# Choice of keys and levels of linear attention beside the projections' tiles, and attention's scores three heads ahead

## The reference, cut to what matters

```python
h = rms_norm(x, norm1_g)
(qa, ka, va, qi, ki, wi, qb, kb, vb, rb, gl, uc) = split_cols(h @ w_in)
# qa, ka, qi, ki are rotated by position (partial_rope)
# a) attention, 8 heads, over chosen keys: per block of 128 queries
score = sum_h wi * relu(qi @ ki.T) * IDX_SCALE          # 4 index heads
_, idx = lax.top_k(where(causal, score, -inf), 128)     # n_keep = min(256, 512 // 4)
o_a = softmax(where(valid, q @ k[idx].T * ATTN_SCALE, -inf)) @ v[idx]
# b) gated linear attention, 4 heads: S_t = diag(a_t) S_{t-1} + k_t^T v_t, o_t = q_t S_t,
#    log a = log_sigmoid(gl @ w_gate_up + b_gate) / 16; then rms norm, times silu(rb)
# c) multiscale_pool(uc)
x = x + concat([o_a, o_b, o_c]) @ w_out
x = x + conv_glu_ffn(rms_norm(x, norm2_g))
```

## Time and profile before

| what | us |
| --- | --- |
| median of three runs (5285.48 to 5310.4) | 5291.39 |
| the profiled execution, its own time | 5324.58 |
| its span, first to last instruction | 5322.7 |
| first layer: projections | 18.07 to 209.22 |
| first layer: mixers | 209.22 to 428.40 |
| second layer: projections | 963.78 to 1154.82 |
| second layer: mixers | 1154.82 to 1379.63 |

### The profile page before, as it was taken

One profiled execution on the slowest core, in us unless ns is written; L12 is line 12 of the kernel. 1 busy time (PEld: TensorE's weight loads), 2 busy tenths in 40 slices (PEclk: granted clock), 3 DMA queues, 4 the chain that ended last, 5 costly groups with the idle time before them and its releaser, 6 DMA issues.

```text
span 5322.7 us, 63196 instructions
## 1 busy us (share of the span) xinstructions
PE 4985.8 (94%) x27502; PEld 2773.6 (52%) x27502; DVE 1481.4 (28%) x2779; ACT 1077.8 (20%) x2068; POOL 324.2 (6%) x302
## 2 busy tenths in 40 slices
PE   9879999987899999999998988888999999989999
PEld 4444444444444444665554567777544555544444
DVE  2362210227211010000224346664310334410100
ACT  1121000012100012110214133333211333311210
POOL 1110000101000000000004100000000001000000
PEclk9879999987899999999999999998999999989999
DMA  3222222223122111111134322210311000101211
GB/s 130 87 111 79 72 71 77 75 79 121 70 79 74 67 57 63 48 48 48 60 127 133 130 66 72 69 54 26 125 52 54 18 26 26 41 31 65 87 71 56
DMA packets 91842, 378.39 MB, mean 71 GB/s; under 512 B 7984, under 2 KB 33712, under 8 KB 62128
## 3 DMA queue, kind: packets, MB, share of 16 engines
q1 hardware_dynamic: 80608, 332.92, 17.6%
q0 software_dynamic: 9808, 37.75, 2.1%
q10 hardware_dynamic: 1152, 3.67, 0.2%
HBM read 334.46 MB, written 39.85 MB: 70 GB/s over the span
## 4 chain that ended last, share of the span: by engine, by line
PE 70%; DVE 4%; ACT 2%; issue 2%; DMA 0%; POOL 0%; POOLq 0%; DVEq 0%; ACTq 0%
PE ps L521 29%; PE ps L333 21%; PE ps L542 5%; PE ps L3335 2%; PE ps L1748 2%; PE ps L3262 1%; PE ps L339 1%; PE ps L3346 1%; PE ps L2445 1%; PE ps L3265 1%; PE ps L3261 1%; PE ps L2395 1%; PE ps L948 1%; PE ps L3263 1%; PE ps L1779 0%
## 5 line engine op out<-in xcount | busy, mean ns | idle before, releaser
L521 PE MATMUL ps<-A,W 128*128 128x512 f32 (+1 forms) x5408 | 2178.4, 563 | 23.4 <-DVE A L1670 6.2
L521 PEld LDWEIGHTS ps<-A,W 128*128 128x128 f32 x5408 | 1032.6, 192 | 1126.4 <-issue 1084.3
L333 PE MATMUL ps<-A,W 64*64 64x64 f32 (+3 forms) x3264 | 710.3, 386 | 44.5 <-DVE R L2886 13.8
L333 PE MATMUL ps<-A 64*64 64x64 f32 (+3 forms) x8416 | 510.5, 246 | 73.2 <-ACT A L3488 23.2
L333 PEld LDWEIGHTS ps<-A,W 128*128 128x128 f32 (+2 forms) x3264 | 397.3, 168 | 337.9 <-issue 308.7
L333 PEld LDWEIGHTS ps<-A 64*64 64x64 f32 (+2 forms) x8416 | 467.8, 155 | 182.3 <-issue 103.7
L542 PE MATMUL ps<-W,A 128*128 128x512 f32 (+1 forms) x896 | 366.7, 572 | 2.2 <-ACT A L1534 2.2
L542 PEld LDWEIGHTS ps<-W,A 128*128 128x128 f32 x896 | 173.5, 194 | 193.6 <-issue 187.8
L435 ACT ACTIVATE A<-R 128x512 f32<-128x512 f32 (+1 forms) x96 | 52.6, 574 | 790.3 <-DVE R L1544 356.0
L1664 DVE SCALAR_TENSOR_TENSOR A<-ps,V,A 128x512 f32<-128x512 f32 (+1 forms) x48 | 31.0, 660 | 486.9 <-PE ps L333 486.3
L1544 DVE SCALAR_TENSOR_TENSOR R<-ps,MOD,R 128x512 f32<-128x512 f32 (+1 forms) x48 | 31.7, 662 | 440.8 <-PE ps L521 439.5
(11 more groups left out here) (356 smaller groups left out, 4253.9 us busy)
## 6 DMA issues: line engine op xcount, KB each, us to landing
W<-in_ada SPq DMA_DIRECT2D x48, 1024.0 KB, 5.4
W<-in_w_up SPq DMA_DIRECT2D x44, 1024.0 KB, 4.8
W<-in_w_down SPq DMA_DIRECT2D x32, 704.0 KB, 4.0
W<-in_w_in SPq DMA_DIRECT2D x18, 1024.0 KB, 4.8
W<-in_sgu_v SPq DMA_DIRECT2D x16, 1024.0 KB, 4.8
W<-in_sgu_u SPq DMA_DIRECT2D x16, 1024.0 KB, 4.8
W<-in_sgu_z SPq DMA_DIRECT2D x16, 1024.0 KB, 4.8
W<-in_sgu_o SPq DMA_DIRECT2D x16, 1024.0 KB, 4.8
```

What stands on the lines that cost most here:

```text
L333: r = e.matmul(out, a, b, start=start and i == 0, stop=stop and i == len(pairs) - 1, skip_group_check=loose)
L521: t = e.matmul(ps, w[:, k, c:c + mc], x(k, seg), start=k == 0, stop=k == kt - 1)
```

## The change

The diff does these things, in both layers of the first block.

* The tiles of the projections get the order qi (2), ki, gl and wi, qb, kb, qa (4), ka (4), uc (2), rb (2); then vb (4 tiles), then va (4). So w_vb is loaded ahead of w_va. They use banks 0 to 3 alone.
* From tile 5 (kb) on, each of the 21 tiles has a place `beside` it: for block j = 1 to 3, seven tiles, of which the first holds the four index heads and the next six the rounds of the choice (3, 3, 3, 3, 2, 2), and each of the 21 one step of linear attention. These use banks 4 to 7. The barrier between projections and mixers is gone, and buffers are laid so that these parts may overlap: `b.h` lies on `b.mix`, `b.tmp` on `b.pr`, the gate's scratch on `b.pt`, and each query block has its own mask.
* The mixers' turns run from -3 to 31. PE makes the transposes of t first and then the scores of t + 3; ACT and DVE are two ahead. `index` and `chosen` are gone from the turns, and linear attention starts there at its step 22, the chunk 2 of 4.
* POOL's two window averages (`pool_mix`) come after all its products for linear attention.

```diff
+QI, KI, GL, GQ, GK, QA, KA, UC, RB, VB, VA, TILES = 0, 2, 3, 4, 5, 6, 10, 14, 16, 18, 22, 26
+ROPED = (0, 1, 2, 6, 7, 8, 9, 10, 11, 12, 13)
+FIRST = 5
+ROUNDS = (3, 3, 3, 3, 2, 2)
+def beside_tile(m):
+    return ((m - FIRST) // 7 + 1, (m - FIRST) % 7) if m >= FIRST else (0, 0)
 def block1_sp(pl, e, l):
...
+    slab_load(pl, e, ("w_vb", l), ins["w_vb"][l])
     for i in range(2):
         slab_load(pl, e, ("w_va", l, i), ins["w_va"][l, i])
-    slab_load(pl, e, ("w_vb", l), ins["w_vb"][l])
...
+    def beside(m, seg=None):
+        r = m - 1
+        if r in ROPED:
+            ps = take(pl, ("rot", l, r), ring)
+            e.wait_ge(*S_.act_projected.at(l, r))
+            e.wait_ge(*free(pl, ("rot", l, r)))
+            e.matmul(ps[:, :], table(pl, "rot"), b.dest[r], start=True, stop=True).then_inc(
+                *S_.rotated.next((l, r)))
+        j, part = beside_tile(m)
+        if j:
+            for hh in range(4 if part == 0 else 0):
+                index(j, hh)
+            next(strand)
...
-    end(pl, ("proj", l), "pe")
-    mixers_pe(pl, e, l)
+    mixers_pe(pl, e, l, strand)
...
+    for m in range(TILES):
+        if m < VB and m not in (GL, GQ):
...
+        j, part = beside_tile(m)
+        if j:
+            for hh in range(4 if part == 0 else 0):
+                index(j, hh)
+            next(strand)
+    mixers_act(pl, e, l, strand)
...
-    end(pl, ("proj", l), "dve")
-    for event in ends(pl, ("proj", l)):
-        e.wait_ge(*event)
-    mixers_dve(pl, e, l)
+        j, part = beside_tile(m)
+        if j:
+            for hh in range(0 if part else 4):
+                index_dve(pl, e, l, j, hh)
+            next(strand)
+            if part:
+                select_dve(pl, e, l, j, part - 1)
+    mixers_dve(pl, e, l, strand)
...
-TURNS = range(-2, 33)
-ROUNDS = (3, 3, 2, 2, 2, 2, 2)
+TURNS = range(-3, 32)
...
-            if x == "s" and 0 <= t + 1 < 32:
-                scores(t + 1)
+            if x == "s" and 0 <= t + ahead < 32:
+                scores(t + ahead)
...
-            elif x == "i":
-                for hh in heads:
-                    index(j, hh)
-            elif x == "r" and 0 <= t < 24 and t % 8 < 7:
-                chosen(t // 8 + 1, t % 8)
...
-    mixers(pl, e, l, scores, turned_, index, nothing_of, gla_pe, ada, pooled, nothing_of, weighed, "stiagow")
+    mixers(strand, scores, 3, turned_, ada, pooled, nothing_of, weighed, "tsagow")
...
-    mixers(pl, e, l, scores, turned_, index, nothing_of, gla_act, ada, pooled, nothing_of, weighed, "stigaow")
+    mixers(strand, scores, 2, turned_, ada, pooled, nothing_of, weighed, "stgaow")
...
-    mixers(pl, e, l, scores, nothing_of, index, chosen, gla_dve, ada, nothing_of, probs, nothing_of, "sriagp")
+    mixers(strand, scores, 2, nothing_of, ada, nothing_of, probs, nothing_of, "sagp")
...
-def mixers_pool(pl, e, l):
+def gla_pool(pl, e, l):
...
-        if lev == 1:
-            pool_mix(pl, e, l, 0)
+        yield
+        yield
...
-    pool_mix(pl, e, l, 1)
+    yield
```

More of the change, by code:

```diff
@@ L548, in tokens_pe @@
                 pl.slab_freed[key] = S.projected.last()
+        if beside is not None:
+            beside(i)
 def merged(work):
@@ L654, in block1_pe, with index @@
         inputs_in(pl, e)
[L656 to L663, removed]
+    strand = gla_pe(pl, e, l)
+    ring = "0123"
+    def index(j, hh):
+        L, o, at = P * (j + 1), 64 * (hh % 2), ("index", l, j, hh)
+        ps = take(pl, at, "4567")[:, 0:L]
+        if (j, hh) == (1, 0):
+            e.wait_ge(*S_.roped.at(l, KI))
+        e.wait_ge(*free(pl, at))
+        e.matmul(ps, b.qi[o:o + 64, hh // 2, P * j:P * j + P], b.ki[o:o + 64, 0:L], start=True, stop=True).then_inc(
+            *S_.index_scores.next((l, j, hh)))
+    def beside(m, seg=None):
[11 more added lines that the diff above has]
+            next(strand)
     h = lambda k, s: b.h[:, k, :]
[L666 removed]
+    features_pe(pl, e, ("w_in", l), [("w_in", l, 0)], 8, 256, h, [(0, S)], beside=beside, ring=ring,
                 ready=lambda k, s: S_.normed.at(("n1", l), k, SC))
[L668 to L670 removed]
+    features_pe(pl, e, ("w_in", l), [("w_in", l, 1)], 8, 256, h, [(0, S)], begun=KI, keep=True, beside=beside, ring=ring)
+    wv = slab(pl, ("w_in", l, 1), 2048, 8)
+    ps = take(pl, ("wi", l), "4567")
     e.wait_ge(*free(pl, ("wi", l)))
@@ L789, in block1_pool @@
     e.memset(b.uc[:, :, 0:16], 0.0).then_inc(*S_.pool_zeroed.next(("uc", l)))
+    strand = gla_pool(pl, e, l)
     e.wait_ge(*S_.rope_ready.at(l, "c"))
[L791 to L795, removed]
-        e.wait_ge(*event)
-    mixers_pool(pl, e, l)
+    for x in b.uy:
+        e.memset(x[:, 0:16], 0.0).then_inc(*S_.pool_gla.next())
+    for m in range(TILES):
+        r = m - 1
+        if r in ROPED:
+            e.wait_ge(*S_.rotated.at(l, r))
+            e.tensor_tensor(b.dest[r], b.dest[r], b.CT, ALU.mult).then_inc(*S_.pool_roped.next((l, r)))
+        if beside_tile(m)[0]:
+            next(strand, None)
+    pool_mix(pl, e, l, 0)
+    pool_mix(pl, e, l, 1)
     end(pl, ("mixers", l), "pool")
@@ new lines, in select_dve @@
+def select_dve(pl, e, l, j, part):
+    S_, b, L, wrote = pl.S, pl.b1[l], P * (j + 1), pl.S.dve_wrote
+    sc, wk = b.sc[:, 0:L], b.wk[:, 0:L]
+    if part == 0:
+        e.wait_ge(*S_.index_summed.last())
+        e.tensor_tensor(sc[:, L - P:L], sc[:, L - P:L], table(pl, "causal"), ALU.add).then_inc(*wrote.next())
+    for rnd in range(ROUNDS[part]):
+        src = sc if part == 0 and rnd == 0 else wk
+        e.wait_ge(*wrote.last())
+        e.max(b.m8, src).then_inc(*wrote.next())
+        e.wait_ge(*wrote.last())
+        e.match_replace(wk, b.m8, src, USED).then_inc(*wrote.next())
+    if part == len(ROUNDS) - 1:
+        e.wait_ge(*wrote.last())
+        e.tensor_scalar(b.bias[j], wk, USED, NEG, ALU.not_equal, ALU.mult).then_inc(*S_.selected.next((l, j)))
```

207 lines of the change are left out of this document (91 added, 116 removed).

## The result

| what | us |
| --- | --- |
| median before (5285.48 to 5310.4), the runs beside those of after included | 5300.65 |
| median after (5159.72 to 5183.07) | 5172.74 |
| the profiled execution of after, its own time and its span | 5159.72, 5157.9 |

The ratio is 0.976, with a 95% interval of 0.9723 to 0.9797: 128 us less. The forecast was 5190 us, 101 less, with a range of 5135 to 5255.

The account below looks back on a forecast made before the run. PE was taken to bound the projections, each turn's chain and a low clock the mixers. Projections 218.6 plus mixers 141 gave 359.6 us per layer against 410.3, 101 less for two layers: 5190 us, range 5135 to 5255.

Parts of the forecast that it names:

- Projections: Projections stage, per layer: 191.15 us plus 18 of moved PE work, 6.5 of waits and 3 for the clock, 218.6.
- the part that was put at 3.6 us: PE work moved beside the tiles: linear attention's gate, one transposition and the first of four chunks, estimated at 3.6 us.
- The waits: PE's waits in projections: second index group 1.5 us, last level 2, keys' transposition 1, second chunk 2; 6.5 in all.
- DVE's load: DVE in the projections: busy time up to some 120 us, the moved work fitting beside the tiles at some 80% load.
- the rival: Beside the tiles DVE becomes late, partly through POOL contention: two us at 21 places, 5255 us, or 5290; chance 0.12.
- Mixers, work that stays: Mixers: of PE's 117 us at full clock 18 move beside the tiles and 99 stay.
- Mixers, waits: Mixers: PE waits about 8 us at the start, 3 at the norm, 3 in the last three turns; 14 together.
- The doubt about a drain: Start of the mixers: by the skill page table switches drain 1.38 us each, making the forecast 5.6 us later.
- Mixers, the clock: Mixers: PE's granted clock rises from 0.73 to 0.78, so 99 us of work take 127.
- The rival of the full clock: Mixers: denser PE work keeps 2.4 GHz, 75 us less per layer, 5140 us; chance 0.18.
- The chain not shortened: Mixers' turns: PE still late by one engine each turn, mixers 165 us, 5238 us in all; chance 0.18.
- half clock throughout: Mixers: PE stays at 1.2 GHz, mixers 208 us, 5324 us in all, slower by 0.6%; chance 0.07.

Follow-up runs that it names:

- Experiment 5: The changed kernel with each max of the choice made twice on DVE, beside the tiles; 5177.76 us, ratio 0.9757 to the kernel before.
- experiment 6: The changed kernel with DVE's division ahead of its step of linear attention in each turn; 5166.23 us, ratio 0.9748 to the kernel before.
- experiment 7: The changed kernel with the spread rows of the norm before the projections in banks 4 to 7; 5164.99 us, ratio 0.9743 to the kernel before.
- 1: The changed kernel with scores one head ahead again on all engines, the moved work still beside the tiles; 5218.71 us, ratio 0.9848 to the kernel before.
- 3: The changed kernel with linear attention back in the turns, only the choice beside the tiles; 5243.92 us, ratio 0.9895 to the kernel before.
- 4: The changed kernel with index scores and choice back in the turns, only linear attention beside the tiles; 5229.49 us, ratio 0.9863 to the kernel before.
- experiment 9: The changed kernel with six idle DVE max instructions before the divisions of pairs 13, 20 and 26; 5189.57 us, ratio 0.9793 to the kernel before.

## Why the prediction was right, and where its sizes were off

**Projections, forecast 218.6, measured 217.59 and 217.46: right in the sum, and partly by luck.** PE's busy time was to be 191.15 + 18 + 3 for the clock, 212.2; it is 211.93. The two terms behind it were both off. The granted clock did not fall against before: it is 0.97 against 0.96, and in the second layer 0.96 against 0.95. Busy time times clock, added up over windows of 1 us, gives 184.3 us of work at full clock before and 205.1 after, 20.8 more (181.4, 202.4 and 21.0 in the second layer). So the moved work took some 21 us and not 18, and the 3 us for the clock did not come; the two errors cancel. Most of the first is the part that was put at 3.6 us: gate, transposition and chunks take 6.0 (1.09 at 81.26, 0.60 at 212.41, twice 0.59 for L1054, and 1.54 and 1.62 for the products at 227.01 and 237.35), since not one but two chunks have their products there. The mixers lost only some 16 us of work by the same reckoning; why it is 5 us less than what came in here isn't shown.

The waits were to be 6.5; the windows leave 217.59 - 211.93 = 5.7. Three of the four places were right in kind: 2.5 us at a level's product behind ACT's relu of the second index group (forecast 1.5), 1.8 at the last level (2), 1.3 at the second chunk (2), and none at the transposition of the keys (1). The clock behind such a wait is seen in the next group:

```profile
199.20 1.17 PE L1032 MATMUL ps<-A 32*128 32x128 f32 x32 [1.78 <-POOL A L1388]
200.30 12.27 PE L542 MATMUL ps<-W,A 128*128 128x256 f32 x32
200.00:202.00 2.00, 2.00 (x21) 1.59 (x14) 1.61 (x3) 0.00 (x0) 0.00 (x0) 0.69 0.00 0
202.00:204.00 2.00, 2.00 (x6) 1.55 (x6) 1.93 (x6) 0.00 (x0) 0.00 (x0) 0.50 0.00 0
```

The second line joins the last sixteen products of vb, of 256 columns, with the first sixteen of va, of 512. Such groups take 3.72 us (at 193.69) and 7.13 (at 228.49) at full clock, 10.85 together, so the low clock cost some 1.4 us. Most of what the clock takes from the stage stands behind no wait at all: during and behind 64 products of only four columns (10.64 us from 54.09 on, PE busy throughout) the clock is 0.80 and 0.68 in the two windows of 10 us from 51.31 on, and the kernel before has the same at its own 64, which start at 154.08: 0.50 from 158 to 168.

**DVE's load, forecast up to 120 us in the stage: right.** It is 117.52 and 121.89. Where the tiles carry moved work, from 80 to 238.9, DVE is busy 106.4 of 158.9 us, 67% and not the 80% of the forecast. The index sums with 512 keys took 752 ns on average, as against 1.33 us for the two of the earlier trace rows; but POOL was idle while they ran (194.16 to 196.62), so they are no test of the contention that spoke for the rival. A large DVE operation with two inputs that did meet a POOL product, L1325 at 207.62, took 0.92 us, where the eleven operations of the same size in L821 took 0.69. Experiment 5 settles the rival: DVE has room for 25 us more.

**Mixers, work that stays, forecast 99 us: right.** 115.22 x 0.88 is 101.4.

**Mixers, waits, forecast 14 us, measured 12.7: right in the sum.** The start has 6.9 us of idle PE up to 267.5 with the norm within it (forecast 8 and 3, so 4 too many): 1.6 at the chunk that opens the stage, 0.6 at a division, 1.8 at the norm's roots and 2.9 at the division behind the norm's end, which experiment 6 could only push on to ACT's copy. The last three turns wait 1.18, 0.78 and 0.69 us for the copy and w_out 0.52, 3.2 in all (forecast 3). The other 2.6 us are short waits inside the turns, for which nothing was forecast. Only one of the two tables was loaded there, for 1.28 us at 239.31, with ACT idle for another 1.08 us behind it; the silu table had been loaded at 228.90, beside the tiles. The doubt about a drain (the Trainium skill, ScalarE: Activation LUTs, "What ACT_TABLE_LOAD costs") doesn't come into the result, since ACT waits for DVE at that place in any case; the load starts 0.02 us after the ACTIVATE ahead of it, and the 1.08 us behind it are less than the 1.38 that the prediction took from the page, so this load shows no such drain either.

**Mixers, the clock, forecast 0.78, measured 0.88: this is the term that was mis-sized.** 99 / 0.78 was 127 us, measured are 115.2: 12 of the 13 us by which the mixers came out shorter, in each layer. The 0.88 lies above the 0.75 to 0.85 that the prediction named as what the profile would show (and the bare turn of 3.02 us just above its 2.6 to 3). In the other kernels whose mixers are those of after the clock was 0.85 and 0.84 (experiment 5), and 0.81 and 0.89 (7): never as low as 0.78. The stage cut at its joints:

```profile
238.90:249.40 10.50, 8.94 (x37) 5.33 (x35) 4.78 (x18) 4.35 (x14) 0.00 (x0) 0.63 0.32 136
249.40:267.50 18.10, 12.80 (x115) 7.23 (x114) 6.76 (x20) 7.74 (x17) 0.00 (x0) 0.88 0.61 233
267.50:296.00 28.50, 27.67 (x114) 11.53 (x114) 6.30 (x34) 9.19 (x31) 1.33 (x2) 0.67 0.49 181
296.00:366.80 70.80, 65.81 (x409) 36.38 (x409) 22.88 (x86) 28.95 (x75) 7.80 (x8) 1.00 0.59 225
```

I took a mixture of the two levels from the earlier trace rows for the whole stage. What came is both in a row: up to 296, with the short turns of 128 and 256 keys and with waits of 1.6 to 2.9 us, something between 0.63 and 0.88; from there to the end the full level, 2.4 GHz, even over the last turns with their idle gaps up to 1.18 us. The stretch at 359 of before, on which I leaned against the full clock, was no sample of these turns. The rival of the full clock, 5140, was right for the last 71 of 128 us and wrong for the rest.

**The sum.** Forecast were 101 us less in four stages, measured are 135: 26 of the 34 are the mixers' clock and waits in two layers, 2 the projections, and 5.5 the second layer's worse start (415.9 against 410.3), which I had not counted. By medians 128 us are gained and not 135; 3.2 of the difference are the first tile's wait, the rest is no more than what medians of a few runs leave open. That the time itself was met within 17 us, where the gain was 27 us larger than forecast, is luck in part: the forecast started from a median before of 5291.39, and with the later runs it is 5300.65.

**The chain not shortened, 5238, is refuted** by the bare turn of 3.02 us, and half clock throughout by the 0.88. (Two small things in the working: the low clock's share of the mixers before was 160.4 - 117 = 43 us and not 42, and for the 165 us of mixers in this rival no sum is given.)

What stays open is the clock itself. In 1, 3 and 4 (143, 187 and 172 us of mixers) it is 0.75 on average. In after it is full from 296 us on, 57 us behind the stage's start, but in experiment 7's first layer only from 80 us behind the start, with the same instructions and no wait over 0.5 us between 35 and 80 us. The two stages differ at their start by 0.4 us: the products of L1054 take 1.13 us there and 0.70 in after. What in the order of small products holds the clock up or down wasn't separated from the waits.

## What to carry to other kernels

Work of one engine that stands between the steps of another's chain is waited for there; moved beside a stage that another engine fills, it was cheap here (25 us more of it cost 7 and 3.5), and only then did a longer lead pay (42 us against 10). When a ring of banks is narrowed, look at who held its first bank before the stage: that wait stands in no list of what was moved. After a wait is removed, read the group behind it before counting the gain (experiment 6: 2.86 us at the division became 2.77 at the copy). And before a few us in one profiled stage are put down to an edit, look for a kernel in which that stage is unchanged: here such a stage took 126.5 us and 135.3.

## What the runs showed of the hardware

The clock that PE was granted made up some 30% of the mixers' gain: the 160.39 us that PE was busy at 0.73 would have been 133 at the 0.88 of after, and those 27 us are part of the 91 that the first layer's mixers gained. It also differs where nothing was changed: experiment 7's mixers, with the instructions of after, had 0.81 in the first layer and 0.89 in the second, 135.33 and 126.49 us. Waits are followed by a low clock: in experiment 9, set against experiment 7, waits of 2.79 and of 1.57 and 2.78 us lengthened the stage by 5.3 and 10.6. But unbroken work can have a low clock too. These six us of experiment 9 stand ahead of its late division's wait, and experiment 7, which has no late division, is at 0.50 in the six us at the same place in its stage (308.2 to 314.2):

```profile
312.00:318.00 6.00, 6.00 (x23) 1.61 (x23) 0.57 (x2) 0.85 (x4) 0.00 (x0) 0.50 0.16 42
```
